# Layer norms in two VectorE passes, stored by halves, with the first up weights split early into their own buffers

## What is computed

```python
        mix = merged @ w_out[l]
        h = layer_norm(DEEPNORM_ALPHA * h + mix, ln1_g[l], ln1_b[l])
        ffn = (jax.nn.silu(h @ w_ffn_gate[l]) * (h @ w_ffn_up[l])) @ w_ffn_down[l]
        h = layer_norm(DEEPNORM_ALPHA * h + ffn, ln2_g[l], ln2_b[l])
```

## Time and profile before

| | us |
|---|---|
| median of 3 runs (lowest, highest) | 755.26 (754.42, 755.43) |
| the profiled execution | 754.85 |
| its span, first to last instruction | 752.8 |
| busy in the span: TensorE | 736.5 (98%) |
| VectorE | 379.3 (50%) |
| ScalarE | 306.2 (41%) |
| GpSimd | 114.9 (15%) |
| mean granted clock of TensorE | 0.996 |

### The profile page before, as it was taken

How to read it: one execution, slowest core, us unless ns; L and a number is a source line. 1 busy time by engine, 2 the same in 40 slices (tenths; PEclk the granted TensorE clock), 3 DMA queues, 4 the chain that set the end, 5 groups by cost and what they waited for, 6 DMA issues and landing times.

```text
span 752.8 us, 9715 instructions
## 1 busy us (share of the span) xinstructions
PE 736.5 (98%) x3731; PEld 622.6 (83%) x3731; DVE 379.3 (50%) x651; ACT 306.2 (41%) x467; POOL 114.9 (15%) x134
## 2 busy tenths in 40 slices
PE   9999999999999999999999999999999999999994
PEld 7889887888888988888789888888888888888883
DVE  3523297797778784664973312322332243233575
ACT  3513476567767777232343222332232132213511
POOL 2507080523343430000110000000000000000011
PEclk9999999999999999999999999999999999999998
DMA  8425233112101205536312233233323321332202
GB/s 260 154 87 166 60 106 118 57 41 73 57 1 57 56 1 145 191 112 224 111 57 93 76 111 111 64 103 111 111 60 108 111 98 69 112 111 88 79 29 84
DMA packets 57167, 72.73 MB, mean 97 GB/s; under 512 B 3856, under 2 KB 44336, under 8 KB 57136
## 3 DMA queue, kind: packets, MB, share of 16 engines
q1 hardware_dynamic: 57136, 72.32, 30.0%
HBM read 70.21 MB, written 2.10 MB: 96 GB/s over the span
## 4 chain that ended last, share of the span: by engine, by line
PE 89%; DVE 6%; ACT 2%; issue 2%; DMA 0%; POOLq 0%; POOL 0%; ACTq 0%; DVEq 0%
PE ps L1280 79%; PE ps L1292 4%; PE ps L1288 3%; PE ps L1289 3%; DVE stat L1164 1%; DVE y L1189 1%; DVE wl L885 1%; ACT y L826 1%; DVE prob L1102 1%; ACT wh L596 1%; DVE ptl L895 0%; DMA arena<-in_x 0%; DVE y L1192 0%; DVE y L1169 0%; DVE wl L895 0%
## 5 line engine op out<-in xcount | busy, mean ns | idle before, releaser
L885 DVE TENSOR_TENSOR wl<-stage,wh 128x2048 fp32r<-128x2048 f32 (+1 forms) x49 | 111.9, 2284 | 206.9 <-ACT wh L602 177.6
L1280 PE MATMUL ps<-wh,xh 128*128 128x512 f32 (+1 forms) x384 | 148.0, 386 | 0.0
L1280 PE MATMUL ps<-wh,xl 128*128 128x512 f32 (+1 forms) x384 | 146.5, 382 | 0.0
L1280 PE MATMUL ps<-wl,xh 128*128 128x512 f32 (+1 forms) x384 | 146.4, 381 | 0.0
L1280 PE MATMUL ps<-ath,wh 128*128 128x512 f32 (+1 forms) x384 | 146.1, 380 | 0.0
L1280 PE MATMUL ps<-atl,wh 128*128 128x512 f32 (+1 forms) x384 | 146.0, 380 | 0.0
L1280 PE MATMUL ps<-ath,wl 128*128 128x512 f32 (+1 forms) x384 | 146.0, 380 | 0.0
L602 ACT CAST wh<-stage 128x2048 fp32r<-128x2048 f32 x37 | 70.5, 1906 | 166.4 <-PE ps L1280 166.4
L1280 PEld LDWEIGHTS ps<-atl,wh 128*128 128x128 f32 x384 | 72.2, 188 | 13.8
L1280 PEld LDWEIGHTS ps<-ath,wl 128*128 128x128 f32 x384 | 72.2, 188 | 13.7
L1280 PEld LDWEIGHTS ps<-wh,xl 128*128 128x128 f32 x384 | 72.1, 188 | 13.9
(11 more groups left out here) (240 smaller groups left out, 1037.1 us busy)
## 6 DMA issues: line engine op xcount, KB each, us to landing
stage<-in_w_in SPq DMA_DIRECT2D x28, 512.0 KB, 4.6
stage<-in_w_ffn_gate SPq DMA_DIRECT2D x22, 512.0 KB, 4.7
stage<-in_w_ffn_up SPq DMA_DIRECT2D x22, 512.0 KB, 4.5
stage<-in_w_ffn_down SPq DMA_DIRECT2D x22, 512.0 KB, 3.8
stage<-in_w_out SPq DMA_DIRECT2D x8, 512.0 KB, 4.6
arena<-in_x SPq DMA_DIRECT2D x8, 256.0 KB, 5.6
stage<-in_w_in SPq DMA_DIRECT2D x8, 256.0 KB, 5.9
stage<-in_w_branch_nsa SPq DMA_DIRECT2D x4, 512.0 KB, 7.0
```

The lines of the kernel that those rows point to most:

```text
L885: dve.tensor_tensor(wl[:, slot, 0:n], stage[slot][:, 0:n], wh[:, slot, 0:n].bitcast(fp32), ALU.subtract).then_inc(w_lo, 1)
L1280: return pe.matmul(out, (sh, sh, sl)[i], (mh, ml, mh)[i], start=start and i == 0, stop=stop and i == 2)
```

## The change

The norm no longer uses ScalarE and GpSimd for the tile's columns. The mean is subtracted and gamma multiplied in one VectorE pass, in four quarters of 256 columns, and the reciprocal root is multiplied and beta added in another, in two halves of 512. The four quarters stand between the small steps, each of which waits only for the small step before it. ScalarE keeps the square root. In the tail the last tile is stored in two halves, each as soon as its own `h_ok` has come; `h_ok` now means left and right half. The first moments of each tile follow its partial add at once. The first up weights get buffers of their own, `second_h` and `second_l`, over tiles 6 to 13 of `fact`; their high half is made after the first root, their low half behind the variance of the third tile. `ht_lo_of(0)` now stands after the second tile's norm, `ht_lo_of(1)` behind the new low half.

```diff
-    BIAS_COLS = 704
...
-        sb("fact_before", [P, FT - 8, SEQ], fp32, early)
+        sb("fact_before", [P, FT - 16, SEQ], fp32, early)
+        second_h = sb("second_h", [P, 2048], f32r, early)
+        second_l = sb("second_l", [P, 2048], f32r, early)
...
-            def __call__(self, ins):
+            def later(self, ins):
                 ins.then_inc(self.s, 1)
                 self.n = self.n + 1
+
+            def __call__(self, ins):
+                self.later(ins)
                 self.eng.wait_ge(self.s, self.n)
...
-            for m in range(MT):
+            for m in range(MT - 1):
                 for h in h_ok:
                     sp.wait_ge(h, MT + m + 1)
                 sp.dma_start(out_d[:, m, :], y[:, m, :]).then_inc(stored, 16)
-            sp.wait_ge(stored, 16 * MT)
+            m = MT - 1
+            for half in range(2):
+                c = slice(512 * half, 512 * half + 512)
+                sp.wait_ge(h_ok[half], MT + m + 1)
+                sp.dma_start(out_d[:, m, c], y[:, m, c]).then_inc(stored, 16)
+            sp.wait_ge(stored, 16 * (MT + 1))
...
-            for k in range(2 * MT):
-                ln, m = divmod(k, MT)
-                pool.wait_ge(scaled, k + 1)
-                pool.tensor_tensor(y[:, m, BIAS_COLS:D], y[:, m, BIAS_COLS:D], lnb[:, ln, BIAS_COLS:D],
-                                   ALU.add).then_inc(h_ok[1], 1)
...
                 act.activation(nrm[:, m, 1:2], nrm[:, m, 0:1], ACT.Sqrt).then_inc(sq_ok, 1)
-                act.activation(y[:, m, :], y[:, m, :], ACT.Identity, bias=nrm[:, m, 4:5]).then_inc(centred, 1)
...
             root(0)
+            split_to(second_h[:, :], U_FFN + 1, 1, U_BRANCH)
             root(1)
             ht_hi_of(0)
+            ht_hi_of(1)
             root(2)
-            ht_hi_of(1)
-            late_split(U_FFN + 1, 1)
+            ht_hi_of(2)
             root(3)
-            ht_hi_of(2)
             ht_hi_of(3)
...
-                dve.tensor_scalar(nrm[:, m, 4:5], mv[:, m, 0:1], -1.0, None, ALU.mult)
...
-                step(dve.reciprocal(n[:, 2:3], n[:, 1:2]))
...
-                dve.tensor_tensor(y[:, m, 0:BIAS_COLS], y[:, m, 0:BIAS_COLS], lnb[:, ln, 0:BIAS_COLS],
-                                  ALU.add).then_inc(h_ok[0], 1)
+                def centre(quarter):
+                    c = slice(256 * quarter, 256 * quarter + 256)
+                    step.later(dve.scalar_tensor_tensor(out=y[:, m, c], in0=y[:, m, c], scalar=mv[:, m, 0:1],
+                                                        in1=lng[:, ln, c], op0=ALU.subtract, op1=ALU.mult))
+
+                centre(0)
                 dve.wait_ge(sq_ok, k + 1)
+                step.later(dve.reciprocal(r, root))
+                at = step.n
+                centre(1)
+                dve.wait_ge(dve_step, at)
+                step.later(dve.scalar_tensor_tensor(out=t, in0=r, scalar=v, in1=r, op0=ALU.mult, op1=ALU.mult))
+                at = step.n
+                centre(2)
+                dve.wait_ge(dve_step, at)
+                step.later(dve.tensor_scalar(t, t, -0.5, 1.5, ALU.mult, ALU.add))
+                at = step.n
+                centre(3)
+                dve.wait_ge(dve_step, at)
+                step(dve.tensor_tensor(t, t, r, ALU.mult))
+                for half in range(2):
+                    c = slice(512 * half, 512 * half + 512)
+                    dve.scalar_tensor_tensor(out=y[:, m, c], in0=y[:, m, c], scalar=t, in1=lnb[:, ln, c],
+                                             op0=ALU.mult, op1=ALU.add).then_inc(h_ok[half], 1)
...
                 add_rows(m, 0, m).then_inc(mg_lo, 1)
+                dve.wait_ge(mg_lo, KD + m + 1)
+                moments(m, 0)
             split(U_OUT + 3, 1)
-            dve.wait_ge(mg_lo, KD + MT)
-            for m in range(MT):
-                moments(m, 0)
...
                 variance(m)
                 if m == 2:
+                    split_to(second_l[:, :], second_h[:, :], U_FFN + 1, 1)
+                    ht_lo_of(1)
+                norm(m)
+                if m == 1:
                     ht_lo_of(0)
-                    ht_lo_of(1)
-                if m == 3:
-                    split(U_FFN + 1, 1)
-                norm(m)
...
-                     (w8(wh, 1), w8(wl, 1))]
+                     for pair in ((first_h, first_l), (second_h, second_l))]
```

More of the change, by code:

```diff
@@ L322, in build_layer @@
         x2_arrived, ln_arrived = sem("x2_arrived"), sem("ln_arrived")
-        var_ok, sq_ok, centred, scaled = sem("var_ok"), sem("sq_ok"), sem("centred"), sem("scaled")
+        var_ok, sq_ok = sem("var_ok"), sem("sq_ok")
         h_ok = [sem("h_ok0"), sem("h_ok1")]
@@ L1170, in add_rows, with variance @@
                                                 op1=ALU.add)
-            def variance(m):
-                step(dve.bn_aggr(mv[:, m, :], stat[:, m, :, :].rearrange("p a b -> p (a b)")))
-                dve.tensor_scalar(nrm[:, m, 4:5], mv[:, m, 0:1], -1.0, None, ALU.mult)
+            def variance(m, groups=None):
+                groups = stat[:, m, :, :] if groups is None else groups
+                step(dve.bn_aggr(mv[:, m, :], groups.rearrange("p a b -> p (a b)")))
                 dve.tensor_scalar(nrm[:, m, 0:1], mv[:, m, 1:2], EPS, None, ALU.add).then_inc(var_ok, 1)
@@ L1180, in norm @@
                 ln, m = divmod(k, MT)
-                n = nrm[:, m, :]
-                dve.wait_ge(sq_ok, k + 1)
-                step(dve.reciprocal(n[:, 2:3], n[:, 1:2]))
-                step(dve.scalar_tensor_tensor(out=n[:, 3:4], in0=n[:, 2:3], scalar=n[:, 0:1], in1=n[:, 2:3],
-                                              op0=ALU.mult, op1=ALU.mult))
-                step(dve.tensor_scalar(n[:, 3:4], n[:, 3:4], -0.5, 1.5, ALU.mult, ALU.add))
-                step(dve.tensor_tensor(n[:, 3:4], n[:, 3:4], n[:, 2:3], ALU.mult))
@@ L1188, in norm @@
-                dve.wait_ge(centred, k + 1)
-                dve.scalar_tensor_tensor(out=y[:, m, :], in0=y[:, m, :], scalar=n[:, 3:4], in1=lng[:, ln, :],
-                                         op0=ALU.mult, op1=ALU.mult).then_inc(scaled, 1)
-                dve.wait_ge(scaled, k + 1)
-                dve.tensor_tensor(y[:, m, 0:BIAS_COLS], y[:, m, 0:BIAS_COLS], lnb[:, ln, 0:BIAS_COLS],
-                                  ALU.add).then_inc(h_ok[0], 1)
+                v, root, r, t = [nrm[:, m, c:c + 1] for c in range(4)]
@@ L1616, in ffn_tile @@
                 return last
-            views = [tuple(t[:, :].rearrange("p (k n) -> p k n", k=8) for t in (first_h, first_l)),
-                     (w8(wh, 1), w8(wl, 1))]
+            views = [tuple(t[:, :].rearrange("p (k n) -> p k n", k=8) for t in pair)
+                     for pair in ((first_h, first_l), (second_h, second_l))]
             h_transposed_at = {(0, 1): 2, (1, 1): 3}
```

## The result

| | before | changed |
|---|---|---|
| median of 6 runs each, same chip, us | 754.80 (754.42 to 755.43) | 751.04 (750.29 to 752.31) |
| ratio, 95% interval | | 0.995 (0.9937 to 0.9963) |
| profiled execution / its span | 754.85 / 752.8 | 751.33 / 749.6 |

A forecast was written before the change was run, and what follows sets the result against it. TensorE was taken to bound the kernel, leaving its first-layer-norm pauses (0.97 us) and the tail (1.60) to win. The 2.57 us gain took 754.85 to 752.3, 752.7 by the median; forecast 752.5, range 751.4 to 754.2.

The forecast's parts named there:

- What bounds the kernel: TensorE is busy almost throughout; only its pauses (3.10 us, first layer norm) and work behind its last matmul can be won.
- The new norm: On VectorE, from aggregate to tile ready: 3.81 us instead of 4.78, with quarters of 0.48 and small instructions hidden behind them.
- nothing overlaps: Rival: VectorE instructions do not overlap, each norm loses 0.64 us, gain 0.0, so 754.9; chance 0.09.
- quarters as dear as halves: Rival: 256 columns on VectorE cost what 512 do, 0.75 us; 1.75 us slower, 756.6; chance 0.03.
- The first layer norm: TensorE's pauses there fall from 3.10 to 2.12 us (0.15, 1.39, 0.58, none at tile 3): gain 0.97.
- the same shapes: nothing: The up weights' matmuls on TensorE read other buffers at the same shapes, so no time change was claimed.
- The moved pieces: Moved copies, loads and casts around the first layer norm: mostly at no cost, except that second_l delays tile 1's ht_lo.
- a new pause: TensorE waits 1.39 us before the feed-forward for tile 1's ht_lo, leaving 0.2 of the 1.6 won before.
- The tail: Behind the last matmul: norm ready 0.95 us earlier, store in halves 0.65 shorter, together 1.60.
- The sum: First layer norm 0.97 plus tail 1.60 gives a gain of 2.57 us.
- The range: 751.4 to 754.2 us, from a quarter pass costing 0.44 to 0.56 us, plus half a microsecond between runs on the fast side.
- nobody else had their time: Removing ScalarE's centring and GpSimd's eight additions frees time that no other work had been denied.

The follow-up runs named there:

- uncut: The changed kernel with the centring pass whole (1024 columns) in front of the root's small steps instead of in quarters: 750.95 us against 754.90 for the kernel before.
- norm_only: The kernel before with the new norm alone; moments, order, up weights and stores as before: 752.12 us against 754.68 for the kernel before.
- later_and_half: The changed kernel, first four transposes waiting for the left half alone, second_l behind the third tile's norm: 749.61 us, ratio to the kernel before 0.9933.
- after_again: The changed kernel run once more, unaltered: 751.45 us against 754.65 for the kernel before.

## Why the prediction was wrong

By its own steps:

- **What bounds the kernel**: right. The stage of the first layer norm and the work behind the last matmul are all that the change moved in the span, and the ledger's 337.3 us between them stood still. In the stage 0.21 of 1.35 us were no pauses, as told below.
- **The new norm**: right to 0.07 us a norm. Quarter 0.48 as estimated, overlap of 0.08 as read from the earlier trace rows, so the rivals "nothing overlaps" and "quarters as dear as halves" fell. The section quoted for the first (the Trainium skill, VectorE: DVE Perf Modes, "The DRAIN you can't avoid") itself adds that an instruction that is not held starts earlier, so it and these rows do not contradict each other. The warning against passes below 512 columns (the Trainium skill, VectorE: DVE Perf Modes, "The TRN2 errata") was not empty: going against it did no harm, but uncut shows that the cut won nothing. Its estimate of about 3.7 us from quarter 0 to the norm's end met 3.43 (364.58 to 368.01), against my 3.50. My sentence that every small instruction hides behind a quarter was true and worth nothing, and I had not worked out the uncut form beside it.
- **The first layer norm**: each pause was named, with its place and its releaser, to 0.15 us. The term was mis-sized all the same: 0.97 forecast, 1.35 measured in the stage. Pauses explain 1.14 of it, 0.17 more than forecast. The other 0.21, of which 0.18 lie behind tile 3's transposes, is mostly the spacing of the 128x256 matmuls, which the sum took as fixed ("the same shapes: nothing"): 0.1177, 0.1189 and 0.119 for 24, 48 and 120 of them before, 0.1136, 0.1178 and 0.1178 after. By count that is 0.29, but the first of the 24 is now followed only after 0.22 us, as the first matmul behind a pause or behind transposes is in all these kernels, and that gives 0.10 back. Why the spacing changed is not shown.
- **The moved pieces**: the sum never priced them apart from the norm. Beside the new norm they gave 0.01, and the copy second_l made the largest pause that was left. That was in the forecast as "a new pause"; that it undid what the earlier start had won was shown only by norm_only and later_and_half.
- **The tail**: 1.60 forecast, 1.69 measured. The norm gave 1.06 instead of 0.95, the halves 0.62 instead of 0.65.
- **The sum**: 1.35 + 1.69 = 3.04 in the span, where 2.57 was forecast. **What failed outright is a term that the sum did not have**: the time around the span, about 2.09 before and about 1.73 after, 0.36 us. I had carried it over as a constant. With it the systematic gain is 3.4 us. The medians say 3.76 here and 3.20 in after_again, and over all 63 runs of the kernel before and all 11 of the changed one 3.44; the difference is within what the start wanders.
- **The base**: 752.5 was counted from about 755.07, between the profiled execution and the median of three runs; with six runs the median is 754.80, 0.27 lower. The rivals' times were counted from 754.85 instead, so they stand 0.2 too low beside the forecast. The miss of 1.46 us is thus 0.27 of base, 0.38 of stage, 0.09 of tail, 0.36 around the span, and 0.36 that no part of the ledger has.
- **The range**: its lower end allowed for a cheaper quarter and for scatter, and bounded neither the stage's pace nor the time around the span. A half microsecond more below would have held the result. That this median fell outside is partly bad luck: after_again's, 751.45, lies just inside. That the gain is larger than the 2.57 forecast is not luck, since all 11 runs give the 3.44 above.

"nobody else had their time", said of GpSimd's and ScalarE's work, missed that GpSimd's additions had taken turns with VectorE's. It cost the sum nothing: the 4.78 and 4.76 us that the old norm was priced at are measured and hold that wait.
